# First attention layer: a pair's eight score pieces grouped into five steps of four key tiles

## The reference

```
q = rms_norm(q); gates = sigmoid(h @ w_gate)                 # three gates per head
p_c = masked_softmax(q @ k_cmp.T * scale - slopes * distance)  # 31 compressed keys
p_s = masked_softmax(q @ k_s.T * scale - slopes * distance)    # selected keys
p_w = masked_softmax(q @ k_w.T * scale - slopes * distance)    # window of 512 keys
o = gates[0] * p_c @ v_cmp + gates[1] * p_s @ v_s + gates[2] * p_w @ v_w
return o @ w_out
```

## Time and profile before

| | us |
|---|---|
| median of 3 runs (2265.2 to 2270.03) | 2265.28 |
| the profiled execution | 2267.4 |
| its span, first to last instruction | 2265.6 |
| busy: PE / DVE / ACT / POOL | 2181.6 / 1326.0 / 763.5 / 53.5 |
| busy share: PE / DVE / ACT | 96% / 59% / 34% |
| mean granted TensorE clock | 0.975 |

### The profile page before, as it was taken

One profiled execution on the slowest core, in us unless ns is written; L12 is line 12 of the kernel. 1 busy time (PEld: TensorE's weight loads), 2 busy tenths in 40 slices (PEclk: granted clock), 3 DMA queues, 4 the chain that ended last, 5 costly groups with the idle time before them and its releaser, 6 DMA issues. The chain is left out here.

```text
span 2265.6 us, 34396 instructions
## 1 busy us (share of the span) xinstructions
PE 2181.6 (96%) x13901; PEld 1788.6 (79%) x13901; DVE 1326.0 (59%) x2433; ACT 763.5 (34%) x1443; POOL 53.5 (2%) x33
## 2 busy tenths in 40 slices
PE   8999999999999999999999999999999999799996
PEld 8996668888878977877777878887888788578884
DVE  5257875544454677564445554666556665665657
ACT  5346772111100366311110005333442343355443
POOL 1110000000000300000000000000000000000000
PEclk9998999999999999999999998999999999889998
DMA  5220002222222320122222211111111110212211
GB/s 190 104 102 2 1 2 75 93 93 95 94 89 87 107 79 20 57 93 93 93 93 93 93 68 71 57 57 56 56 56 56 56 56 0 91 38 93 75 38 38
DMA packets 25156, 158.85 MB, mean 70 GB/s; under 512 B 2784, under 2 KB 3296, under 8 KB 7520
## 3 DMA queue, kind: packets, MB, share of 16 engines
q1 hardware_dynamic: 24768, 157.24, 19.7%
q10 hardware_dynamic: 288, 0.20, 0.0%
HBM read 155.33 MB, written 2.10 MB: 69 GB/s over the span
## 5 line engine op out<-in xcount | busy, mean ns | idle before, releaser
L220 PE MATMUL ps<-late_parts,panel_upper 128*128 128x512 f32 x960 | 387.6, 404 | 8.6 <-DVE late_parts L216 5.2
L221 PE MATMUL ps<-late_parts,panel_upper 128*128 128x512 f32 x960 | 382.5, 398 | 0.0
L222 PE MATMUL ps<-late_parts,panel_parts 128*128 128x512 f32 x960 | 380.9, 397 | 0.0
L220 PE MATMUL ps<-hT_parts,panel_upper 128*128 128x512 f32 x736 | 303.7, 413 | 6.3 <-PEq L3398 3.8
L220 PE MATMUL ps<-panel_upper,hT_parts 128*128 128x256 f32 (+2 forms) x964 | 299.9, 311 | 7.4 <-DVE h_lower L896 7.4
L216 DVE TENSOR_TENSOR panel_parts<-panel_sb,panel_upper 128x2048 fp32r<-128x2048 f32 (+1 forms) x152 | 288.2, 1896 | 18.9 <-ACT panel_upper L710 8.3
L221 PE MATMUL ps<-h_lower,panel_upper 128*128 128x512 f32 x736 | 296.3, 403 | 0.0
L222 PE MATMUL ps<-hT_parts,panel_parts 128*128 128x512 f32 x736 | 294.0, 399 | 0.0
L222 PE MATMUL ps<-panel_upper,h_lower 128*128 128x256 f32 (+2 forms) x964 | 286.3, 297 | 0.0
L221 PE MATMUL ps<-panel_parts,hT_parts 128*128 128x256 f32 (+2 forms) x964 | 285.3, 296 | 0.0
L220 PEld LDWEIGHTS ps<-late_parts,panel_upper 128*128 128x128 f32 x960 | 182.1, 190 | 55.3 <-issue 10.2
(11 more groups left out here) (438 smaller groups left out, 2988.3 us busy)
## 6 DMA issues: line engine op xcount, KB each, us to landing
panel_sb<-ffn_gate_up_w SPq DMA_DIRECT2D x44, 1024.0 KB, 4.8
panel_sb<-gdn_w SPq DMA_DIRECT2D x24, 1024.0 KB, 4.8
panel_sb<-ffn_down_w SPq DMA_DIRECT2D x22, 1024.0 KB, 4.8
panel_sb<-nsa_w SPq DMA_DIRECT2D x13, 1024.0 KB, 5.7
panel_sb<-gla_w SPq DMA_DIRECT2D x12, 1024.0 KB, 4.8
panel_sb<-gdn_out_w SPq DMA_DIRECT2D x8, 1024.0 KB, 4.8
panel_sb<-nsa_out_w SPq DMA_DIRECT2D x4, 1024.0 KB, 4.8
panel_sb<-mla_out_w SPq DMA_DIRECT2D x4, 1024.0 KB, 4.8
```

Source lines behind the costliest of these rows:

```text
L220: mm(out, w_hi, x_hi, start=start, stop=False)
L221: mm(out, w_hi, x_lo, start=False, stop=False)
L222: return mm(out, w_lo, x_hi, start=False, stop=stop)
```

## The change

A pair's eight pieces are packed into five steps that each hold exactly four key tiles, since (1+3), 4, (2+2), 4 and (1+3) tiles make up the 20. There are 40 steps in place of 64. A step's transposes are one group of eight and its copy is one of 1024 columns. Scores, bias, exponential and weighting still go piece by piece, at column offset `at`; the reciprocal takes the sums of all pieces of a step at once. `psum` and `pmin` have four columns in place of two. The places of the extras in the rounds are given anew.

```diff
-    STEP_ORDER = [(0, 0), (2, 0), (3, 0), (3, 1), (1, 0), (2, 1), (0, 1), (1, 1)]
+    STEP_PIECES = [[(0, 0), (2, 0)], [(3, 0)], [(1, 0), (1, 1)], [(3, 1)], [(0, 1), (2, 1)]]
...
-            for c in range(0, n, PIECE):
-                keys = slice(c, min(c + PIECE, n))
-                for ab in range(2):
-                    r = head_rows(ab)
-                    last = mm(ps[:, 2 * (v % 2) + ab, keys], qT[r, pair, tok(t)], kT[r, br * GROUPS + pair // 2, keys], start=True, stop=True)
+            for t, br, at, n in pieces:
+                for c in range(0, n, PIECE):
+                    end = min(c + PIECE, n)
+                    for ab in range(2):
+                        r = head_rows(ab)
+                        last = mm(ps[:, 2 * (v % 2) + ab, at + c:at + end], qT[r, pair, tok(t)], kT[r, br * GROUPS + pair // 2, c:end], start=True, stop=True)
...
-                for kt in range(t + 1):
-                    last = nc.tensor.transpose(ps[:, 4 + ab, tok(kt)], prob[v % NB][:, ab, tok(kt)], ident[:])
+                for tile in range(TT):
+                    last = nc.tensor.transpose(ps[:, 4 + ab, tok(tile)], prob[v % NB][:, ab, tok(tile)], ident[:])
...
-            nc.scalar.copy(pT[v % 2][:, :, 0:n], ps[:, 4:6, 0:n]).then_inc(S("n_pT"), 1)
+            nc.scalar.copy(pT[v % 2][:, :, :], ps[:, 4:6, :]).then_inc(S("n_pT"), 1)
...
-            nc.vector.reciprocal(psum[b][:, :], psum[b][:, :]).then_inc(S("n_inv"), 1)
+            sums = psum[b][:, 0:2 * len(pieces)]
+            nc.vector.reciprocal(sums, sums).then_inc(S("n_inv"), 1)
...
-            if v == 5:
+            if v == 3:
                 cmp_bias(3)
-            if v == 7:
+            if v == 4:
                 cmp_weights(3)
...
-            if v % 3 == 0 and 12 <= v < 60:
-                lower_out(v // 3 - 4)
+            if v % 2 == 0 and v >= 8:
+                lower_out((v - 8) // 2)
```

More of the change, by code:

```diff
@@ L284, in build_in @@
     n_inv = [take(TT, GROUPS) for _ in range(2)]
-    psum, pmin = [take(2) for _ in range(NB)], [take(2) for _ in range(NB)]
+    psum, pmin = [take(4) for _ in range(NB)], [take(4) for _ in range(NB)]
     prob = [take(2, T) for _ in range(NB)]
@@ L381, in pair_step, with ops_before @@
         pair, rest = divmod(v, PAIR_STEPS)
-        t, br = STEP_ORDER[rest]
-        return pair, t, br, (t + 1) * P
+        pieces, at = [], 0
+        for t, br in STEP_PIECES[rest]:
+            pieces.append((t, br, at, (t + 1) * P))
+            at += (t + 1) * P
+        assert at == T
+        return pair, pieces
+    def ops_before(v):
+        return sum(2 * len(STEP_PIECES[u % PAIR_STEPS]) for u in range(v))
     def head_rows(ab):
@@ L596, in scores @@
         def scores(v):
-            pair, t, br, n = pair_step(v)
+            pair, pieces = pair_step(v)
             if v == 0:
@@ L639, in values @@
             pe.wait_ge(S("n_pT"), v + 1)
[L640 to L644, removed]
+            for t, br, at, n in pieces:
+                for kt in range(t + 1):
+                    for ab in range(2):
+                        of = br * KV_COLS + pair // 2 * DH
+                        last = mm(ps[head_rows(ab), bank, tok(t)], vtok[:, kt, of:of + DH], pT[v % 2][:, ab, at + kt * P:at + (kt + 1) * P],
+                                  start=False, stop=br == 1 and kt == t, skip_group_check=True)
             last.then_inc(S("n_valued"), 1)
@@ L837, in exps @@
         def exps(v):
[L838 to L842, removed]
+            pair, pieces = pair_step(v)
+            k = 0
+            for t, br, at, n in pieces:
+                for ab in range(2):
+                    act.wait_ge(S("n_biased"), ops_before(v) + k + 1)
+                    nc.scalar.activation(prob[v % NB][:, ab, at:at + n], prob[v % NB][:, ab, at:at + n], ACT.Exp, bias=pmin[v % NB][:, k:k + 1],
+                                         scale=-1.0, accum_out=psum[v % NB][:, k:k + 1]).then_inc(S("n_exp"), 1)
+                    k += 1
         def turned(v):
-            pair, t, br, n = pair_step(v)
             act.wait_ge(S("n_turned"), v + 1)
@@ L869, in act_nsa @@
                 upper_o(v // PAIR_STEPS - 1)
-            if v == 3:
+            if v == 2:
                 save_pc(2)
-            if v == 6:
+            if v == 4:
                 cmp_exp(3)
-            if v == 8:
+            if v == 5:
                 save_pc(3)
-            if v % 12 == 10 and v // 12 < 4:
-                upper(N_OUT + v // 12)
+            if v % 8 == 6 and v < 32:
+                upper(N_OUT + v // 8)
         upper_o(NPAIR - 1)
```

48 lines of the change are left out of this document (27 added, 21 removed).

## The result

After: 2254.08 us, median of 4 runs (2251.84 to 2255.95); before, on the same chip, 2267.52 us (2265.2 to 2270.03). The ratio is 0.9942, with a 95% interval of 0.9928 to 0.9956: 13.4 us less. Forecast were 2255.3 us and a gain of 10.0 (11.2 was measured against the median of 2265.28 that the forecast started from). The profiled execution took 2254.1 us where the forecast had 2257.4; its span is 2252.2, at a mean clock of 0.974.

What follows compares the result with a forecast made beforehand. No engine full, TensorE nearest; the loss is TensorE waiting for weighting when bias, an extra and weighting share a step. -11.4 - 2.8 + 1.2 - 0.5 + 3.5 = -10.0, from 2265.28 to 2255.3 us; range 2250 to 2262.

Steps and rivals of the forecast that it cites:

- term 1: Pairs 1 to 6: five packed steps a pair, alternating 17.71 and 18.96 us, 110.0 against 121.4: -11.4 us.
- term 2: Last pair: no next scores to make, so its last values end at 16.1 us against 18.95: -2.8 us.
- term 3: Start, ahead of the loop: eight tiles of work instead of four, first transposes at 170.0 us: +1.2 us.
- terms 4 and 5: Pair 0: closer-packed compressed branch, 30.0 us against 30.5 (-0.5), and two half-clock stretches of 1.75 us (+3.5).
- The walk: Step-by-step timing of TensorE and VectorE from trace durations; T starts when TensorE is ready or .05 us after weighting.
- The rival that VectorE sets the pace: Pairs 1 to 6 and the last: steps of about 3.8 us, pairs 19 to 19.3, total 2259 to 2261; chance 0.20.
- The price of the six-matmul S: Two-piece scores of one and three tiles on TensorE: taken as 1.07 us; the load-based estimate was 1.28.
- The second gap on TensorE: Pair 0, ahead of T(5): TensorE idle for 2.9 us behind VectorE's compressed weights and W(5).

Runs made afterwards that it cites:

- reordered form: Kernel before, still eight steps a pair and nothing packed, with its pieces in the order of the kernel after: 2271.67 us, ratio 1.002 to before.
- after again: The changed kernel run once more with no edit: 2255.17 us, ratio 0.994 to before.
- two copies: Kernel after, with each step's ScalarE copy of 128x1024 made as two of 128x512, one per head: 2253.38 us, ratio 0.9935 to before.
- extras moved: Kernel after, with VectorE's output lowering and 16 panel lowerings moved to steps where the weighting is of one piece: 2252.31 us, ratio 0.9935 to before.
- a reciprocal each: Kernel after, with one reciprocal for each piece instead of one per step: 2253.89 us, ratio 0.994 to before.
- earlier branch: Kernel after, with the last compressed scores ahead of step 3's transposes and the last compressed exponential ahead of step 4's copy: 2247.8 us, ratio 0.9921 to before.
- fastest: Kernel after, with the compressed branch earlier, extras at light steps and each ScalarE cast split in four: 2242.21 us, ratio 0.9897 to before.
- six steps: Kernel after, with the two pieces of two key tiles as steps of their own again, casts and lowerings re-placed: 2265.9 us, ratio 0.999 to before.
- the last experiment: Kernel with compressed branch earlier, extras moved and casts quartered, its 16 VectorE panel lowerings replaced by four on GpSimd: 2254.59 us, ratio 0.9939 to before.

## Why the prediction was right, and where not

The median was met to 1.2 us, and so closely by luck. Two misses had opposite signs, pair 0 with its clock (7.3 us too little gained) and the program behind the steps (3.5 us given back that the forecast did not have), and a third thing helped: the forecast took 2.1 us off for the profiled execution being slower than the median, which held for before (2267.4 to 2265.28) but not for after (2254.1 to 2254.08). Against the profiled execution the forecast was 3.3 us off (2257.4). Each step against the spans (2265.6 and 2252.2 us), from matmul to matmul:

| step of the forecast | forecast | measured |
|---|---|---|
| term 1, pairs 1-6 | -11.4 | -10.85 |
| term 2, last pair | -2.8 | -2.64 |
| term 3, first T (169.02 to 169.85) | +1.2 | +0.83 |
| terms 4 and 5, pair 0 with its half clock (30.32 to 26.06) | +3.0 | -4.26 |
| the program behind the steps | 0 | +3.5 |
| sum | -10.0 | -13.4 |

- **Term 1 was right in mechanism and size.** Pairs of 17.71 and 18.94 to 18.95 us (17.71 and 18.96 forecast), and TensorE's longest wait in these pairs at the fourth step of every other one, 1.23 us. The 0.55 missing is pair 1's first step, with L546. That the loss lies in whole steps, not in one engine's work, is shown by three doses: TensorE's 7.7 us of added work cost 3.9, a sixth step 7.7, the extras moved to light steps gained 3.5. The walk gave all three within 2 us. A reading of busy time would mislead here: in these pairs TensorE is busy 9.87 us less than before (101.52 for 111.39) and idle 0.98 less, which would credit its work with nearly the whole gain, while the dose gives work on it half its weight. Not separated is what the new places of the extras brought: no run of eight steps has them moved alone, and with five steps moving them was worth 3.5 us, so a part of the 10.85 may be theirs.
- **The rival that VectorE sets the pace** is refuted for these pairs: 110.55 us against 19 to 19.3 each, 114 or more. (Its total was summed a little low: 19 to 19.3 a pair give term 1 as -7.4 to -5.6, and 2260 to 2262, not 2259 to 2261.) Against ScalarE's fewer copies as the source of the gain speaks one small dose, 1.53 us of added work that cost nothing.
- **The price of the six-matmul S** was taken rightly: 1.08 us, against 1.07 taken and 1.28 by the estimate from the Trainium skill (TensorE: Matmul & The Clock Gate, section LDWEIGHTS). The measurement decides. What the estimate had wrong is the sum rather than the price of a load: it put the twelve loads one behind the other, and in the trace twelve loads of 186 ns on the mean pass within 0.96 us, those of the two heads starting within 0.01 us of each other.
- **Term 4** had the mechanism and a wrong ground under it. VectorE's two waits came as forecast (2.25 and 2.41 us), as did the step times: T(3) to T(4) 7.97 us (7.9 forecast), T(4) to T(5) 6.18 at full clock (6.2). Taking the waits out gave 4.5 us in pair 0, 0.9 of it by the clock. The second gap on TensorE came as 1.17 us, not 2.9, because the half clock drew out TensorE's work ahead of it; at full clock it was 3.00. But the walk to T(3) was made "with TensorE costs doubled until 182.4 us", and after ran that part at full clock: T(3) at 180.88, not 185.9. That is 4.9 of the 7.3 us, counted from the first T. Ten profiles have the same gap of 2.20 us; the half clock behind it lasted nothing in four, 3.4 us in one and 6.8 in five, never the 13.6 of before or the 10.2 of its reordered form. In the seven of them that keep pair 0's order it takes 26.1 to 27.1 us, in the two kernels of eight steps 30.3 and 29.6. So most of the gain in pair 0 comes with the change; why the half clock there is shorter with it stays open.
- **Term 5 was mis-sized.** Two stretches of 1.75 us were priced; the one that came in after lasted 6.8 us and cost 0.9, because TensorE waited for VectorE in it. The Trainium skill (TensorE: Matmul & The Clock Gate, section HAM oscillation) tells of a kernel whose clock fell back anew at every wait of 3 to 5 us. The prediction left that length out and took both its gaps of 2.9 us as paid by it. The traces agree in part, and for shorter gaps: every stretch in pair 0 stands at or behind a gap, but after shows one for gaps of 2.20, 2.86 and 1.17 us, the repeated kernel two.
- **The forecast took the rest of the program as unchanged.** It gave back 3.5 us. The code there is the same instruction for instruction, and its time varies from profile to profile:

| kernel | half clock at the start gap, us | pair 1 | out | rest | half clock in the rest, us |
|---|---|---|---|---|---|
| before | 13.6 | 199.34 | 339.69 | 1925.9 | 94.6 |
| after | 0 | 195.91 | 322.77 | 1929.4 | 111.5 |
| after again | 6.8 | 198.11 | 324.98 | 1931.9 | 111.3 |
| two copies | 6.8 | 198.11 | 325.10 | 1925.1 | 97.9 |
| extras moved | 3.4 | 198.54 | 322.09 | 1928.6 | 107.7 |
| a reciprocal each | 0 | 196.33 | 323.71 | 1928.2 | 107.7 |
| earlier branch | 0 | 191.67 | 318.53 | 1926.8 | 101.0 |
| fastest | 0 | 192.16 | 314.38 | 1925.1 | 101.4 |

(The half clock is added up from the granted clock in the traces.) The rest spans 1925.1 to 1931.9 us over kernels that are alike in it, and it tends to be longer the more of it ran at half clock, though not strictly. The ten profiles of the kernels with packed steps that leave the rest as it is have 1927.9 on the mean, before and its reordered form 1925.9 and 1926.6; these two also have the least half clock in it of all thirteen, 94.6 us each. So the better part of the 3.5 us is how the clock fell in these two executions; whether 1 to 2 us of it come with the change stays open.

## What to carry to other kernels

Walk a software pipeline step by step with durations from the trace, and put every engine into it: the walk over TensorE and VectorE alone was exact to 0.02 us in five of six pairs of the changed kernel, and missed by 0.6 in the one that held a group it had left out. With the extras moved it missed by 0.9 in a pair where ScalarE, left out too, decided. What packing saves is steps with their latencies, more than the work removed; what it costs is cover, so look for operations that now follow their input in the same step (here 3.7 us of waits in pair 0, and 0.9 by the clock) and move them one place ahead of the instruction that waits. Extras belong where the following operation is light, and not on GpSimd while VectorE scales tiles in SBUF.

## What the runs showed of the hardware

- The half-clock stretches inside the program came in lengths of 3.4, 6.8, 10.2 and 13.6 us. The same program, with the same gap to 0.01 us, was followed by none in one execution and by 6.8 us in another. In pair 0 and ahead of it, stretches stood at or behind gaps of 1.51 us (six steps) to 3.44 us (six steps, ahead of its T(5)), but none followed a gap of 2.20 us in four executions of ten, nor one of 2.82 us in the pair of the last experiment that ran at full clock.
- What a stretch costs depends on how much TensorE is waited for in it: 0.9 us for 6.8 and nothing for 3.4 between T(4) and T(5), 1.57 for 3.4 in pair 1.
- A GpSimd subtraction in SBUF held up VectorE's scaling in SBUF until it ended, 3.66 us for 1.00 in one weighting and likewise in all four stretches, while VectorE's operations that read PSUM took their usual 0.42 us beside it.
- A second reciprocal of 128x2 right behind the first costs VectorE 0.05 us, and two half copies on ScalarE 0.05 more than the whole one of 128x1024.
